# First attention layer: gate projection tiles set into the attention loop, keys projected last ahead of it, one output bank

## The chip, the cores and the metric

The kernel runs on one core of a Trainium2 chip, in one launch. The metric is the device time in microseconds (us); lower is better.

## What is computed

Four transformer layers over 512 tokens of width 1024, all in float32: an NSA layer (sparse attention with three branches), a differential attention layer, a neighbourhood attention layer and an MLA layer, the last two each with a gated side input. The change touches the NSA layer only. Cut to what matters:

```python
u = rmsnorm(x, g)
q, kc, vc, ks, vs, kw, vw, gate, z = split(u @ w_in)     # 16 heads of 64, 4 key groups
k_cmp, v_cmp = compress(kc), compress(vc)                # 31 blocks, a small MLP
o_c = softmax(q k_cmp + bias) v_cmp
o_s = softmax(q ks + bias) vs       # 8 selected blocks of 64 out of 8: all keys
o_w = softmax(q kw + bias) vw       # window 512: all keys
o = sigmoid(gate) . (o_c, o_s, o_w)
y = (o * silu(z)) @ w_out           # z: 1024 columns, from 1024 features
x = x + rmsnorm(y, g2)
```

## The kernel before

Every matrix product is made of three: a float32 operand is split into a high part (ScalarE's Copy into fp32r) and a low part (raw minus high), and hi*lo, lo*hi and hi*hi are added up in PSUM. SBUF holds all activations; weights stream in *units* of 128x2048 (1 MB) into a ring of three slots (`w_raw`, `w_hi`, `w_lo`). The Sync engine (SP) issues a unit's load as soon as the unit that held the slot is consumed; ScalarE (ACT) makes the high part (`split_high`, L417), GpSimd (POOL) the low part (`split_low`, L426), then TensorE (PE) may use it. Every engine runs a program written by hand, in order; semaphores hold them together. The table `RUNS` (L83 on) gives the order of the units.

**The front of the NSA layer** (`block.tensor`, L2331 on): values, then `nsa_k` in two blocks (first the columns to be compressed, then the keys of both full branches), the first half of the compression (`compress_hidden_tensor`, L1794), the queries in two blocks with the second half between them, the gate logits, and `nsa_z` in two blocks. A block of 512 output columns is 96 matmuls of 128x512. Beside the first z block run the scores against the compressed keys (L1905), on VectorE (DVE) and ACT their softmax meanwhile, and in the last part of the second z block their transposes (`compress_turn_tensor`, L1966). `silu_x` (L683) puts silu(z) into `x`.

**The NSA flow** (`pair_tensor` L1354, `pair_vector`, `pair_scalar`, `pair_pool`): 64 steps, one for each pair of heads (8), half of the queries, branch (2) and query tile; a step has two heads (m) and 128, 256, 384 or 512 keys, and eight steps (one pair of heads) repeat. Step i: PE `scores(i)` (6 matmuls, L1360); DVE adds the bias and takes the maximum (L1460); ACT `exps` (L915); DVE the reciprocal (L1466); POOL `normalise` (L1579); PE `turn` (transposes, L1388, banks 4 and 5); ACT `high` (L1518) and DVE `low` (L1473) take the turned maps out as `u_hi` and `u_lo`; PE `values` for two steps at once (L1407; L1415 adds the compressed branch) into bank 6 or 7. Four steps make a group: ACT `low_out` (L1526), DVE `add_out` (L1480), POOL `gate_out` (times silu(z), split; L1586 to L1596). PE's loop takes two steps at a time: at its turn i it does scores i and i+1, turn i-3, the values of steps i-6 and i-5, turn i-2. ACT's loop does at i: exps(i-1), high(i-3), and `low_out` in every fourth. After the flow `nsa_out` multiplies by w_out; its first chunks (`first_output`) already stand in the flow's last turns.

The differential layer behind it has a flow with projection chunks between its own products (`diff_tensor`, `fill`, `tile_product`, L505): tiles of 128 columns of q, k and z, 8 chunks of 3 matmuls each, in banks 2 and 3 by turns.

## Time and profile before

| what | value |
| --- | --- |
| median of 3 runs | 1393.45 us (1392.7 to 1395.8) |
| the profiled execution's own time | 1394.15 us |
| its span, first to last instruction | 1392.2 us |
| granted TensorE clock, mean | 0.997 |
| busy: PE, ACT, POOL, DVE | 1338.4, 732.5, 765.3, 653.7 us |
| NSA front, continuous on PE | from about 28 to 202.6 us |
| NSA flow: first scores to last values | 202.9 to 360.5 us |
| one pair of heads (8 steps) in the flow | 18.6 us |

A busy time of PE counts a matmul from its start to its modelled end, and these overlap: a 128x512 matmul has a busy time of 0.39 us while the next one starts 0.227 us after it. So PE is read by the distance between starts, and a "busy" of 93% leaves more room than it says.

### The profile page before, as it was taken

The numbers are of one execution on the slowest core, as the hardware profiler recorded it, in microseconds if no ns is written. First come the engines' busy times: TensorE is split into PE (matmuls) and PEld (weight loads), VectorE is DVE, ScalarE is ACT, GpSimd is POOL, SyncE is SP. The second block draws the span as 40 slices with busy tenths as digits, with TensorE's granted clock in tenths as the row PEclk, the third lists the DMA queues.
The fourth block names the chain that finished last, engine by engine and source line by source line (L and its number), as shares of the span: only waits on it lengthen the run. The fifth ranks groups of instructions, "written<-read, shape, count | busy, mean of one in ns | idle before, by whom it ended". The sixth has DMA issues, their size and how long they took to land.

```text
span 1392.2 us, 20871 instructions
## 1 busy us (share of the span) xinstructions
PE 1338.4 (96%) x7738; PEld 1096.1 (79%) x7738; DVE 653.7 (47%) x1609; ACT 732.5 (53%) x1552; POOL 765.3 (55%) x771
## 2 busy tenths in 40 slices
PE   6999999999999999999999999999999999999997
PEld 5888777777888787878788888778889887778885
DVE  4222068888251454553420012881463347887135
ACT  4244258888343556665433233892544356887252
POOL 4455256667554465665652544686646433686652
PEclk9999999999999999999999999999999999999999
DMA  6232311100434222221443222425226222002322
GB/s 240 102 118 95 121 61 32 32 32 2 167 113 145 90 76 99 79 96 44 168 152 139 104 91 91 152 92 197 80 93 225 91 91 61 2 16 105 137 91 61
DMA packets 28324, 138.65 MB, mean 100 GB/s; under 512 B 3520, under 2 KB 4032, under 8 KB 16960
## 3 DMA queue, kind: packets, MB, share of 16 engines
q1 hardware_dynamic: 14624, 98.05, 20.0%
q10 hardware_dynamic: 13600, 39.27, 8.2%
q8 instruction: 63, 1.03, 0.3%
q14 instruction: 37, 0.30, 0.1%
HBM read 127.86 MB, written 8.39 MB: 98 GB/s over the span
## 4 chain that ended last, share of the span: by engine, by line
PE 75%; DVE 8%; POOL 6%; ACT 6%; issue 2%; DMA 2%; ACTq 0%; SPq 0%; POOLq 0%; DVEq 0%
PE psum L471 51%; PE psum L505 9%; DVE w_free L1460 2%; POOL w_free L1579 2%; ACT w_free L915 2%; PE psum L1407 2%; PE psum L1029 2%; PE psum L1388 2%; PE psum L1360 2%; PE psum L1003 2%; ACT u_hi L1518 1%; DVE u_lo L1473 1%; PE psum L725 1%; POOL split L1596 1%; PE psum L1373 1%
## 5 line engine op out<-in xcount | busy, mean ns | idle before, releaser
L426 POOL TENSOR_TENSOR w_lo<-w_raw,w_hi 128x2048 fp32r<-128x2048 f32 (+2 forms) x154 | 415.6, 2714 | 317.6 <-ACT w_hi L417 308.3
L417 ACT ACTIVATE w_hi<-w_raw 128x2048 fp32r<-128x2048 f32 (+1 forms) x90 | 167.1, 1856 | 94.7 <-DMA w_raw<-in_weights 79.5
L471 PE MATMUL psum<-w_hi,split 128*128 128x512 f32 x608 | 195.2, 394 | 3.0 <-POOL w_lo L426 2.2
L471 PE MATMUL psum<-u_lo,w_hi 128*128 128x512 f32 (+1 forms) x492 | 194.1, 395 | 0.0
L471 PE MATMUL psum<-u_hi,w_hi 128*128 128x512 f32 (+1 forms) x492 | 191.7, 390 | 0.0
L471 PE MATMUL psum<-u_hi,w_lo 128*128 128x512 f32 (+1 forms) x492 | 191.7, 390 | 0.0
L915 ACT ACTIVATE w_free<-w_free,neg_max 128x512 f32<-128x512 f32 (+3 forms) x256 | 148.4, 585 | 10.1 <-DVE neg_max L1460 9.1
L1473 DVE TENSOR_TENSOR u_lo<-psum,u_hi 128x512 fp32r<-128x512 f32 (+3 forms) x256 | 123.8, 519 | 28.9 <-ACT u_hi L1518 26.2
L471 PE MATMUL psum<-w_hi,u_lo 128*128 128x512 f32 (+2 forms) x352 | 134.6, 382 | 1.8 <-DVE u_lo L875 1.8
L471 PEld LDWEIGHTS psum<-w_hi,split 128*128 128x128 f32 x608 | 114.2, 188 | 27.5 <-POOL w_lo L426 3.1
L471 PE MATMUL psum<-w_lo,u_hi 128*128 128x512 f32 (+2 forms) x352 | 132.9, 378 | 0.0
L471 PE MATMUL psum<-w_hi,u_hi 128*128 128x512 f32 (+2 forms) x352 | 132.8, 377 | 0.0
L1518 ACT ACTIVATE u_hi<-psum 128x512 fp32r<-128x512 f32 (+3 forms) x256 | 107.9, 463 | 41.8 <-PE psum L1388 38.5
L1388 PE MATMUL psum<-ident,w_free 128*128 128x128 f32 x704 | 110.6, 282 | 17.2 <-POOL w_free L1579 8.1
L471 PE MATMUL psum<-w_lo,split 128*128 128x512 f32 x304 | 118.4, 389 | 0.0
L1388 PEld LDWEIGHTS psum<-ident,w_free 128*128 128x128 f32 x704 | 75.7, 140 | 47.7 <-POOL w_free L1579 27.7
L1579 POOL TENSOR_SCALAR w_free<-w_free,inv 128x256 f32<-128x256 f32 (+1 forms) x128 | 73.2, 586 | 64.2 <-DVE inv L1466 64.2
L471 PEld LDWEIGHTS psum<-u_lo,w_hi 128*128 128x128 f32 (+1 forms) x492 | 91.8, 187 | 20.5 <-issue 0.7
L471 PEld LDWEIGHTS psum<-u_hi,w_hi 128*128 128x128 f32 (+1 forms) x492 | 91.8, 187 | 20.1
L471 PEld LDWEIGHTS psum<-u_hi,w_lo 128*128 128x128 f32 (+1 forms) x492 | 91.9, 187 | 19.1
L1407 PE MATMUL psum<-u_lo,split 128*128 128x256 f32 (+1 forms) x416 | 102.9, 284 | 0.0
L1579 POOL TENSOR_SCALAR w_free<-w_free,inv,gate 128x256 f32<-128x256 f32 (+3 forms) x128 | 76.5, 608 | 43.1 <-DVE inv L1466 43.0
(216 smaller groups left out, 2503.6 us busy)
## 6 DMA issues: line engine op xcount, KB each, us to landing
w_raw<-in_weights SPq DMA_DIRECT2D x87, 1024.0 KB, 4.8
x<-x_scratch ACTq DMA_DIRECT2D x12, 512.0 KB, 5.2
gain<-in_gains ACTq DMA_DIRECT2D x9, 512.0 KB, 4.7
gain<-in_strips ACTq DMA_DIRECT2D x16, 256.0 KB, 2.9
spare<-in_strips ACTq DMA_DIRECT2D x16, 256.0 KB, 3.0
x_scratch<-x ACTq DMA_DIRECT2D x8, 512.0 KB, 4.1
gain<-in_near ACTq DMA_DIRECT2D x8, 512.0 KB, 4.3
w_raw<-in_near ACTq DMA_DIRECT2D x8, 512.0 KB, 3.7
```

The costliest lines, as they stand in the source:

```text
L417: high = nc.scalar.activation(w_hi[b][:, c], w_raw[b][:, c], ACT.Copy)
L426: low = nc.gpsimd.tensor_tensor(w_lo[b][:, c], w_raw[b][:, c], w_hi[b][:, c].bitcast(F32), ALU.subtract)
L471: mm = nc.tensor.matmul(dst, lhs, rhs, start=(a == 0 and k == 0 and (wl, ul) == (0, 1)), stop=(a + 1 == u and k + 1 == nk and (wl, ul) == ...
L505: mm = nc.tensor.matmul(bank(tiles.bank(t)), w[b][:, c:c + P], u[:, k * T:(k + 1) * T], start=(k == 0 and nth == 0), stop=(k == KC - 1 and ...
L915: nc.scalar.activation(p_map(f, i, m, n), p_map(f, i, m, n), ACT.Exp, scale=-1.0, bias=stat_of(neg_max, i, m), accum_out=stat_of(row_sum, ...
L1003: mm = nc.tensor.matmul(bank(m, n), lhs, split[64 * m:64 * m + 64, b:b + n], start=(nth == 0), stop=(nth == 2))
L1029: mm = nc.tensor.matmul(head_bank(d, r), turned_place(i, n, low)[:, pt], split[:, a + v:a + v + P], start=(kt == 0 and nth == 0), stop=(kt ...
L1388: tr = nc.tensor.transpose(psum[:, 4 + m, kt * P:(kt + 1) * P], p_map(f, i, m, n)[:, kt * P:(kt + 1) * P], ident[:])
L1407: mm = nc.tensor.matmul(dst, value_place(f, d, m, kt), pt_pair(buf, pt_step(f, 2 * d) // 2, m, a, b), start=(br == 0 and m == 0 and kt == ...
L1473: nc.vector.tensor_tensor(u_lo[:, c], bank(4 + m, n), u_hi[:, c].bitcast(F32), ALU.subtract).then_inc(f.low, 1)
L1518: nc.scalar.activation(u_hi[:, pt_cols(pt_step(f, i), m, n)], bank(4 + m, n), ACT.Copy).then_inc(f.high, 1)
L1579: nc.gpsimd.tensor_scalar(p_map(f, i, m, n), p_map(f, i, m, n), stat_of(inv, i, m), factor_of(f, i, m), ALU.mult, ALU.mult).then_inc(f.p, 1)
```

## The change

- `nsa_k` is cut in two: `nsa_kc` (compressed columns) stays first, then q0, both halves of the compression back to back, the gate logits, q1, and `nsa_k` (keys) last. The compressed scores run beside and behind q1, their softmax while the keys are projected.
- `nsa_z` is no block any more but 8 tiles of 128 columns, 8 chunks of 3 matmuls (128x512) each, all through PSUM bank 7 (`z_fill`). Six chunks stand ahead of the flow; then in each turn of PE's loop one chunk stands behind the scores and one behind the turns. ACT takes a tile out with Silu (`z_take`), between exps(8t+1) and high(8t-1); the next tile's first chunk waits for that (`z_taken`). ACT splits half a unit for each tile (128x1024), POOL two pieces of 128x512.
- The flow's outputs use bank 6 alone (`out_bank`), so a group's values wait for the group before to be added out. The turned maps move to `x` and to ring slots, since u must stay whole for the z tiles; `nsa_out`'s second unit goes to the place of u when z is done. Its first unit is split in four pieces in the last steps of the flow, the second behind it.
- The gate logits' unit is split over 384 columns instead of 2048.

```diff
 _run("nsa_v", 1, (4, 4), 512, "tokens")
-_run("nsa_k", 2, (4, 4), 512, "features")
+_run("nsa_kc", 1, (4, 4), 512, "features")
+_run("nsa_q0", 1, (4, 4), 512, "features")
 _run("nsa_cmp0", 1, (16,), 128, "compress")
-_run("nsa_q0", 1, (4, 4), 512, "features")
 _run("nsa_cmp1", 1, (16,), 128, "compress")
+_run("nsa_gate", 1, (8,), GATES, "features")
 _run("nsa_q1", 1, (4, 4), 512, "features")
-_run("nsa_gate", 1, (8,), GATES, "features")
-_run("nsa_z", 2, (4, 4), 512, "features")
+_run("nsa_k", 1, (4, 4), 512, "features")
+_tiles("nsa_z", [("z", u) for u in range(KC)])
...
+        def out_bank(f, g):
+            return 6 if f is nsa_flow else 6 + g % 2
...
+        Z_FIRST = 6
+        Z_BANK = 7
+        def z_step(t):
+            return max(0, KC * (t + 1) - Z_FIRST - 1) // 2 * 2 + 1
...
+        def z_fill(pe, first, count):
+            b = SLOT[Z_UNIT]
+            for c in range(first, min(first + count, KC * KC)):
+                t, k = divmod(c, KC)
+                if k == 0:
+                    pe.wait_ge(z_ready, t + 1)
+                    if t == 0:
+                        pe.wait_ge(cmp_shifted, 1)
+                    else:
+                        pe.wait_ge(z_taken, t)
+                col = t % 2 * D + k * P
+                for nth, (w, u) in enumerate(((w_hi, u_lo), (w_lo, u_hi), (w_hi, u_hi))):
+                    mm = nc.tensor.matmul(bank(Z_BANK), w[b][:, col:col + P], u[:, k * T:(k + 1) * T], ...)
+                if k == KC - 1:
+                    mm.then_inc(z_done, 1)
...
+        def z_take(act, t):
+            act.wait_ge(z_done, t + 1)
+            if t >= 3:
+                act.wait_ge(nsa_flow.gated, 2 * (t - 2))
+            nc.scalar.activation(z_home(t), bank(Z_BANK), ACT.Silu).then_inc(z_taken, 1)
...
     def values(d, m):
-                if m == 0 and br == 0 and g >= 2:
-                    pe.wait_ge(f.out_sum, 2 * g - 2)
+                held = 1 if f is nsa_flow else 2
+                if m == 0 and br == 0 and g >= held:
+                    pe.wait_ge(f.out_sum, 2 * (g - held) + 2)
...
     in pair_tensor's loop over i = 0, 2, 4, ...
                 for n in steps:
                     scores(n)
+                if f is nsa_flow:
+                    z_fill(pe, Z_FIRST + i, 1)
...
                 if 0 <= i + 1 - LAG < f.steps:
                     turn(i + 1 - LAG)
+                if f is nsa_flow:
+                    z_fill(pe, Z_FIRST + i + 1, 1)
+                    if i == 0:
+                        compress_turn_tensor(pe, 3)
...
     in pair_scalar's loop over i
+                    for t in range(KC):
+                        if t >= 2 and i == z_step(t - 2) + 3:
+                            z_high_part(act, t)
+                    if f.steps - 4 <= i < f.steps:
+                        split_high(act, NSA_OUT, i - f.steps + 4, 4)
                 if 0 <= i - 1 < f.steps:
                     exps(act, f, i - 1)
+                if f is nsa_flow:
+                    for t in range(KC):
+                        if i == z_step(t) + 1:
+                            z_take(act, t)
...
     in pair_pool's loop over i
+                if f is nsa_flow:
+                    for t in range(2, KC):
+                        if i - z_step(t - 2) - 5 in (0, 1):
+                            z_low_part(pool, t, i - z_step(t - 2) - 5)
+                    if f.steps - 3 <= i <= f.steps:
+                        split_low(pool, NSA_OUT, i - f.steps + 3)
+                    if i == f.steps + LAG + 2:
+                        split_low(pool, NSA_OUT + 1)
...
     PE's program
-            project_tensor(pe, "nsa_k")
-            compress_hidden_tensor(pe, 0)
-            project_tensor(pe, "nsa_q0")
-            compress_hidden_tensor(pe, 1)
-            project_tensor(pe, "nsa_q1", between={(0, 0, 2): lambda: compress_heads_tensor(pe)})
-            project_tensor(pe, "nsa_gate", banks=1, base=4)
-            project_tensor(pe, "nsa_z", only=(0,), between=...)
-            project_tensor(pe, "nsa_z", only=(1,), between=...)
+            project_tensor(pe, "nsa_kc")
+            project_tensor(pe, "nsa_q0")
+            compress_hidden_tensor(pe, 0)
+            compress_hidden_tensor(pe, 1)
+            project_tensor(pe, "nsa_gate", banks=1, base=6)
+            project_tensor(pe, "nsa_q1", between=beside_q1)
+            for j in range(NT):
+                compress_scores_tensor(pe, 1, j)
+            project_tensor(pe, "nsa_k")
             pair_tensor(pe, nsa_flow)
```

How the order moves, at three places. **PE in the flow, at its turn i = 8t+2** (L1360 and L1459 are scores, L1388 and L1487 turns, L1407 and L1507 values, L1416 a chunk of z). Before:

```order
L1388 MATMUL psum<-ident,w_free_63 128x128 x6
L1360 MATMUL psum<-split 128x128 x6
L1360 MATMUL psum<-split 128x256 x6
L1388 MATMUL psum<-ident,w_free_63 128x128 x8
L1407 MATMUL psum<-u_lo,split 128x256
```

Now:

```order
L1487 MATMUL psum<-ident,w_free_68 128x128 x6
L1416 MATMUL psum<-u_lo,w_hi_55 128x512
L1416 MATMUL psum<-u_hi,w_lo_59 128x512
L1416 MATMUL psum<-u_hi,w_hi_55 128x512
L1459 MATMUL psum<-split 128x128 x6
L1459 MATMUL psum<-split 128x256 x6
L1416 MATMUL psum<-u_lo,w_hi_55 128x512
L1416 MATMUL psum<-u_hi,w_lo_59 128x512
L1416 MATMUL psum<-u_hi,w_hi_55 128x512
L1487 MATMUL psum<-ident,w_free_68 128x128 x8
```

The first three chunk rows are the last chunk of tile t, the second three the first chunk of tile t+1: the scores of two steps stand between them.

**ACT in the flow, at i = 8t+1 and 8t+2** (L915 and L956 are exps, L1518 and L1630 high, L1526 and L1638 low_out, L1445 the Silu of a z tile). Before:

```order
L1518 ACTIVATE u_hi<-psum 128x384 x2
L1526 ACTIVATE arena<-psum 64x512
L915 ACTIVATE w_free_63,row_sum<-w_free_63,neg_max 128x256 x2
L1518 ACTIVATE u_hi<-psum 128x512 x2
L915 ACTIVATE w_free_63,row_sum<-w_free_63,neg_max 128x128 x2
```

Now:

```order
L1630 ACTIVATE x_r<-psum 128x384 x2
L1638 ACTIVATE arena<-psum 64x512
L956 ACTIVATE w_free_68,row_sum<-w_free_68,neg_max 128x256 x2
L1445 ACT_TABLE_LOAD
L1445 ACTIVATE arena<-psum 128x512
L1630 ACTIVATE x_r<-psum 128x512 x2
L956 ACT_TABLE_LOAD
L956 ACTIVATE w_free_68,row_sum<-w_free_68,neg_max 128x128 x2
```

Behind the same three pieces of work now come a table load and the Silu, and the next exps have a table load of their own.

**ACT in the front**, from q0's last outputs (L604, L645) on; L417 and L467 are high parts of units. Before:

```order
L604 ACTIVATE split<-psum 128x512 x2
L1815 ACT_TABLE_LOAD
L1815 ACTIVATE arena<-arena 128x248
L417 ACTIVATE w_hi_55<-w_raw_61 128x2048
L417 ACTIVATE w_hi_53<-w_raw_59 128x2048
```

Now:

```order
L645 ACTIVATE split<-psum 128x512 x2
L467 ACTIVATE w_hi_56<-w_raw_64 128x384
L467 ACTIVATE w_hi_54<-w_raw_62 128x2048
L1951 ACT_TABLE_LOAD
L1951 ACTIVATE arena<-arena 128x248
L467 ACTIVATE w_hi_55<-w_raw_63 128x2048
L2014 ACT_TABLE_LOAD
L2014 ACTIVATE arena<-psum 48x512
```

The gate unit's split (384 columns) and those of q1's two units (2048) follow one another; before, a block of 96 matmuls stood on PE between any two of the short units.

## Rows read from the trace of the kernel before

**Rows 1.** Busy time by stretch: front, flow, drain (first), one period (second)
```profile
core 0: us, PE busy (x) PEld busy (x) DVE busy (x) ACT busy (x) POOL busy (x), PEclk, DMA share, GB/s
41.94:202.60 160.66, 160.66 (x951) 131.97 (x949) 48.58 (x57) 58.77 (x59) 71.69 (x16) 1.00 0.30 105
202.89:341.60 138.71, 127.88 (x1055) 105.43 (x1054) 117.16 (x449) 121.23 (x376) 97.67 (x160) 0.99 0.08 24
341.60:360.49 18.89, 17.51 (x125) 15.54 (x126) 10.03 (x30) 10.03 (x26) 9.45 (x15) 1.00 0.16 57
...
246.90:265.50 18.60, 17.35 (x146) 14.46 (x146) 15.97 (x60) 16.32 (x52) 13.20 (x22) 1.00 0.10 30
```

**Rows 2.** Chain of waits through the front: start us, us, what
```profile
85.62 3.88 PE psum L1794 x64
89.50 21.98 PE psum L471 x96
...
145.43 1.44 PE psum L1905 x24
...
197.09 0.45 PE psum L1966 x4
```

**Rows 3.** Timeline of PE, part of one period: start us, us, engine line op
```profile
267.10 1.49 PE L1360 MATMUL psum<-split 64*128 64x384 f32 x12
268.52 0.66 PE L1388 MATMUL psum<-ident,w_free 128*128 128x128 f32 x4
...
275.13 1.12 PE L1388 MATMUL psum<-ident,w_free 128*128 128x128 f32 x6 [0.36 <-DVE u_lo L1473]
276.18 0.96 PE L1360 MATMUL psum<-split 64*128 64x128 f32 x12
277.06 1.09 PE L1388 MATMUL psum<-ident,w_free 128*128 128x128 f32 x8
277.91 0.36 PE L1407 MATMUL psum<-u_lo,split 128*128 128x256 f32 x1
...
280.36 0.55 PE L1388 MATMUL psum<-ident,w_free 128*128 128x128 f32 x2
```

**Rows 4.** Timeline of PE inside a projection block
```profile
97.04 0.39 PE L471 MATMUL psum<-u_lo,w_hi 128*128 128x512 f32 x1
97.26 0.39 PE L471 MATMUL psum<-u_hi,w_lo 128*128 128x512 f32 x1
97.49 0.39 PE L471 MATMUL psum<-u_hi,w_hi 128*128 128x512 f32 x1
```

**Rows 5.** Timeline of ACT at the place of the future Silu
```profile
275.68 1.09 ACT L1518 ACTIVATE u_hi<-psum 128x384 fp32r<-128x384 f32 x2 [0.18 <-PE psum L1388]
276.80 0.59 ACT L1526 ACTIVATE arena<-psum 64x512 f32<-64x512 f32 x1
277.42 0.51 ACT L915 ACTIVATE w_free<-w_free,neg_max 128x256 f32<-128x256 f32 x1
...
278.54 1.09 ACT L1518 ACTIVATE u_hi<-psum 128x512 fp32r<-128x512 f32 x2
```

**Rows 6.** Timeline of ACT in the differential layer's flow, around one Silu
```profile
503.39 1.92 ACT L417 ACTIVATE w_hi<-w_raw 128x2048 fp32r<-128x2048 f32 x1
505.33 1.28 ACT L1203 ACT_TABLE_LOAD   x1
506.62 0.60 ACT L1203 ACTIVATE x<-psum 128x512 f32<-128x512 f32 x1
...
507.73 1.28 ACT L1175 ACT_TABLE_LOAD   x1
```

**Rows 7.** Timeline of all engines behind the compression's first half
```profile
91.02 1.92 ACT L417 ACTIVATE w_hi<-w_raw 128x2048 fp32r<-128x2048 f32 x1 [4.76 <-DMA w_raw<-in_weights]
93.02 9.18 POOL L426 TENSOR_TENSOR w_lo<-w_raw,w_hi 128x2048 fp32r<-128x2048 f32 x2 [6.13 <-ACT w_hi L417]
94.41 1.92 ACT L417 ACTIVATE w_hi<-w_raw 128x2048 fp32r<-128x2048 f32 x1 [1.48 <-DMA w_raw<-in_weights]
```

**Rows 8.** Timeline of DVE, adding out a group; of POOL, a 512-column low part
```profile
277.43 0.86 DVE L1480 TENSOR_TENSOR arena<-psum,arena 64x256 f32<-64x256 f32 x2
...
385.64 1.30 POOL L426 TENSOR_TENSOR w_lo<-w_raw,w_hi 128x512 fp32r<-128x512 f32 x1 [1.48 <-DVE x L864]
```

**Rows 9.** Chain of waits through the drain of the flow
```profile
349.20 2.82 PE psum L471 x12
...
358.66 1.83 PE psum L1407 x16
360.49 21.86 PE psum L471 x96
```

More of the change, by code:

```diff
@@ L213, in _program @@
         LAG = 3
+        PT_SET = 14 * P
         MLA_SCALE = (64 + ROPE) ** -0.5
@@ L1352, in scores @@
             def scores(i):
-                if f is nsa_flow and i < 2:
-                    pe.wait_ge(bank_free["act"], 4 + RUNS["nsa_out"]["others"] - 2 + 2 * i)
+                if f is nsa_flow and i == 0:
+                    pe.wait_ge(bank_free["dve"], 4 + RUNS["nsa_k"]["taken"] + 4)
                 if i >= 2:
@@ L1548, in pair_scalar @@
                     high(i - LAG)
-                if i == (f.steps if f is na_flow else f.steps + LAG - 1) and f is not nsa_flow:
+                if i == (f.steps if f is na_flow else f.steps + LAG - 1):
                     split_high(act, RUNS[f.name + "_out"]["unit"] + 1)
@@ L2405, in _ @@
             load_strips(act, nsa_flow, 1)
-            project_scalar(act, "nsa_z", silu_x, only=(0,))
+            project_scalar(act, "nsa_q1", split_features_act(QH + 4 * T, 0.125), halves=True, split_at=1)
             compress_softmax_scalar(act)
-            last_z_scalar(act, "nsa_z", silu_x)
+            z_high_part(act, 0)
+            z_high_part(act, 1)
+            for j in range(NT):
+                act.wait_ge(bank_done, 4 * RUNS["nsa_k"]["block"] + j + 1)
+                nc.scalar.activation(split[:, KH + j * T:KH + (j + 1) * T], bank(j), ACT.Copy).then_inc(split_hi, 1)
+            for g in range(3):
+                compress_turned_high(act, g)
             pair_scalar(act, nsa_flow)
```

241 lines of the change are left out of this document (153 added, 88 removed).

## Prediction

> **What bounds the kernel now.** I read the busy times by stretch first. In the front PE is busy for the whole stretch and the others for less than half [rows 1], and the chain of waits runs through PE alone, block after block [rows 2]: there only PE's work counts. In the flow a period of eight steps takes 18.6 us, with ACT busy for 16.32, DVE 15.97 and POOL 13.20 us of it [rows 1]. PE's busy time (17.35) has to be read by the distance of starts. From the timeline of PE [rows 3]: scores of 384 and 512 keys take 1.42 us (267.10 to 268.52), of 128 and 256 keys 0.88 us (276.18 to 277.06); 8 transposes 0.85 us; 20 value matmuls 2.45 us (277.91 to 280.36), 0.122 each. A period holds two of each kind of scores (4.6 us), 40 transposes (4.2) and 56 value matmuls (6.9): 15.7 us. So PE stands idle for some 2.9 us of a period, 17 us in the six regular periods, in pieces behind DVE and POOL such as the 0.36 us at 275.13 [rows 3]. That is the room into which the change puts z.
>
> **What leaves the front.** Two blocks of 96 matmuls, at 0.227 us from start to start [rows 4]: -43.6 us, all on PE's path. Six chunks of three return ahead of the flow: +4.1 us. One of four groups of transposes (0.45 us [rows 2]) moves into the flow. The other projections, compressed scores (1.44 us a set [rows 2]) and transposes only change places. The softmax that ran beside z has the keys' block (21.8 us) and the six chunks as its cover.
>
> The new order has one place where a unit is late. The compression's halves and the gate logits now follow one another: 3.88 + 3.88 + 24 x 0.227 = 13.2 us on PE from 85.6, so it is ready for q1 at 98.8. q1's first unit takes the slot freed by the first half, at 89.5. In the trace such a load landed at 94.4, its high part took 1.92 us and its low part 4.6 us (9.18 for two) [rows 7]: 100.9. PE waits 2.1 us. For q1's second unit the same chain ends under q1's first half. Front in all: -43.6 + 4.1 - 0.45 + 2.1 = **-37.9 us**.
>
> **What enters the flow.** 58 chunks. A chunk costs 3 x 0.227 = 0.68 us of PE, eight in a period 5.5 us: PE's own work is 15.7 + 5.5 = 21.2 us, already over 18.6. ACT gets one Silu (0.60 us), two table loads (1.28 us each, as around the Silu in the differential flow [rows 6]) and a high part of 128x1024 (bounded by 0.6 and 1.92 us, half of the latter taken, 1.0): 4.2 us, so 20.5 us of work. POOL gets two pieces of 1.30 us [rows 8]: 15.8 us, still covered. DVE gets nothing.
>
> To that comes a new wait. All tiles use bank 7. The last chunk of tile t is issued behind turn(8t-2), the first of tile t+1 two scores later, and waits for the Silu. In between ACT has to work through high(8t-2), low_out, exps(8t+1), a table load, the Silu. In the trace, from the end of that turn (PE goes on at 276.18 [rows 3]) to the end of exps(8t+1) (278.54 [rows 5]) it is 2.36 us; with 1.28 + 0.60 it is 4.24 us. PE can put one chunk (0.69) and the scores (0.88) into it. It waits 2.7 us, with the semaphore 2.8 us. More slack on ACT would not shorten this, because high(8t-2) cannot start before the turn. Behind the Silu ACT in turn waits about a microsecond for chunk and turn(8t-1). A period becomes 21.2 + 2.8 = **24.0 us**. I walked PE and ACT through one period with these durations, and nothing else ended later: the maps for each turn are ready 1 to 4 us ahead. The waits that PE has now vanish under the chunks.
>
> One output bank: values of a new group wait for add_out. Now the adding ends at 278.29 [rows 8], just behind the values' start at 277.91 [rows 3]; with two to three chunks and the wait for the Silu between, the bank is free before it is wanted. Cost 0, with the chunks as cover; without them about 0.4 us in every second group.
>
> **The sum.** Before: 138.7 us from the first scores to scores 62 and 63, then 18.9 us of drain [rows 1]. Now: the opening up to turn 6 of the loop about 13.3 us (8.6 us of scores, transposes and six chunks, a first wait of 2.8 for a Silu, some 2 us in which turn(2) waits for what ACT and DVE still owe to turn(1); before it was 8.5, the 138.7 less seven periods), six periods of 24.0 = 144.0, then the last period with 4 chunks instead of 8 and no wait for a bank, but Silu and table loads on ACT (19.5 us of work there), 20: 177.3 us, +38.6. In the drain POOL has four more pieces of 1.30 us ahead of the first `nsa_out` chunks, which stood there without a stall [rows 9]; they hold PE for about 3 us, of which the drain's own idle time takes back a good part: +1.7 us. The low part of the second unit (4.6 us) lies under the last values and output chunks and ends about 1.5 us before it is needed. Behind the flow all is as it was. -37.9 + 38.6 + 1.7 = **+2.4 us**. Against the profiled execution's own 1394.15 us that is 1396.5; the median shown is 0.7 us lower, so I predict **1395.8 us**. A measurement of this kernel tells a change from none at about 0.2% (2.8 us); this is just inside.
>
> **The rivals.**
> *The cover holds (faster).* If the wait for bank 7 falls into time that PE would lose anyway, a period is PE's work or ACT's, 21.2 or 20.5 us, and with small change 21.5. That takes 2.5 us from each of six periods and from the opening: 17 us less, 1378 us. For it: ACT has now 2.3 us idle in a period and could run ahead. Against it: the chain begins with a turn that PE issues right before its own last chunk. Chance 0.2.
> *ACT becomes the clock (slower).* ACT has 20.5 us of work, and its present waits (18.6 - 16.3 = 2.3 us) are for turns which the chunks make later, not earlier. If they stay, and the wait for turn(8t-1) behind the Silu, with its own chunk and transposes (1.5 to 2 us) and the one bank's 0.4 to 1 us come on top, a period takes 25.5 to 26 us: +11 us in six periods and the opening, 1407 us. It decides from the point at which ACT has no idle time left but behind turns. Chance 0.2.
> *A table load costs more than its record.* In the differential flow the Silu starts 1.29 us after its table load [rows 6], with no gap before the load either: the high part of 1.92 us ends where it starts. If a switch drained ACT for about as long again, each wait would be 1.3 us longer, with seven waits +9 us: 1405 us. Chance 0.02, since these rows show no drain. The Trainium skill ("ScalarE: Activation LUTs", "What ACT_TABLE_LOAD costs") states such a rule: 1283 ns for the load and some 1380 ns of drain, 2.66 us for every switch, and under "Table sets" it says to batch calls by set. By that price the sum would be +12 instead of +2.4 us; the trace agrees with its 1283 ns and not with its drain.
> *The change does not do what it says.* Each engine's order shows the chunks, loads and splits at the places named, so this is not it.
>
> **How the numbers follow.** The walk as it stands: 0.58, with a span of its own of 1390 to 1402 (a wait of 2.5 to 3.3 us seven times, opening and drain 2 us either way, the late unit 0 to 3 us). Of it 0.04 lies below 1390.6, 0.33 within 0.2% of before, 0.21 above. Cover 0.2, all faster; ACT as clock 0.2 and drain 0.02, all slower. So faster 0.24, same 0.33, slower 0.43: the likeliest time lies within the bound, but more of the chance lies above it. The range takes in both large rivals, cut at their near sides: 1379 to 1409.
>
> **What would show it.** PE should reach the flow's first scores near 165 us with one wait of about 2 us for a low part ahead of q1 (L426's counterpart). In the flow seven waits of PE on the Silu of bank 7, 2.5 to 3.3 us each, at a distance of 24 us; ACT with 16 more table loads there and busy for about 20.5 of 24 us; no wait of values on the adding. The last values should end about 2 us later than the 360.5 us of now [rows 9]. The theory is wrong if the waits on the Silu are under a microsecond, if the periods are 21.5 us (cover) or 26 us (ACT), or if the front gains less than 36 us.

## The result, and the profile after

The changed kernel takes **1425.17 us** (median of four runs, 1422.79 to 1431.29) against 1394.62 us in the same session: ratio 1.0226, 95% interval 1.0188 to 1.0264. I had predicted 1395.8 us and a range of 1379 to 1409. The profiled execution took 1422.79 us, with a span of 1421.0 us and a mean granted clock of 0.986 (before: 1394.15, 1392.2 and 0.997). Here and below, times are medians and ratios come from the runs' means, without four slow runs far out (4604.56 us of spread_cmp, 1642.04 us of no_fill, 2641.24 and 1494.69 us of the kernel before).

By stretches, busy times of the changed kernel: front, flow from the first scores to scores 62 and 63, drain, one period at full clock, one with a stretch at half clock (the columns are those of [rows 1]):

```profile
41.94:167.71 125.77, 123.74 (x774) 101.79 (x774) 50.79 (x54) 40.50 (x44) 49.45 (x14) 0.97 0.27 93
167.71:359.91 192.20, 169.18 (x1232) 140.19 (x1232) 120.27 (x451) 152.59 (x405) 109.12 (x170) 0.96 0.13 45
359.91:387.40 27.49, 22.25 (x126) 18.69 (x126) 11.15 (x32) 14.09 (x33) 16.81 (x21) 0.81 0.12 39
207.92:233.18 25.26, 22.25 (x170) 18.42 (x170) 16.20 (x61) 20.43 (x55) 15.77 (x24) 1.00 0.13 42
233.18:260.04 26.86, 23.84 (x170) 19.86 (x170) 16.31 (x61) 20.65 (x55) 15.74 (x24) 0.94 0.13 41
```

| stretch, us | before | predicted | after | miss |
|---|---|---|---|---|
| to the first scores of the flow | 202.89 | 165.0 | 167.71 | +2.7 |
| opening, to scores 6 and 7 | 9.2 | 13.3 | 13.31 | 0 |
| six periods | 110.8 | 144.0 | 157.86 | +13.9 |
| last period | 18.6 | 20.0 | 21.02 | +1.0 |
| drain | 18.9 | 20.6 | 27.49 | +6.9 |
| all behind | 1031.8 | 1031.8 | 1033.6 | +1.8 |

(The opening of before is counted here to the same scores, 6 and 7; my 8.5 us was what 138.7 us leave beside seven whole periods.) Of the 26.3 us of miss, 21.8 stand in the loop and its drain. The 1.8 us behind them come with a stretch of 3.4 us at half of TensorE's clock at 487.1 us, in the next layer, where the trace of before has none. The 0 in the opening is luck: PE waits 0.8 us at its second turn where I had counted some 2, but scores, transposes and chunks take 9.7 us where I had counted 8.6.

**The wait is there, in the size predicted.** PE's waits from the first scores to scores 62 and 63:

```profile
PE psum L1416 <- ACT arena L1445: 11.0, 4, 2.7
PE psum L1416 <- ACT x L1445: 8.3, 3, 2.8
PE psum L1487 <- DVE w_hi L1582: 2.2, 8, 0.8
PE psum L1487 <- DVE w_lo L1582: 0.9, 2, 0.6
```

Seven waits for the Silu, 19.3 us, 2.76 each. One of them and what follows, in the timeline of PE:

```profile
270.14 0.47 PE L1416 MATMUL psum<-u_lo,w_hi 128*128 128x512 f32 x1
270.46 0.39 PE L1416 MATMUL psum<-u_hi,w_lo 128*128 128x512 f32 x1
270.68 0.40 PE L1416 MATMUL psum<-u_hi,w_hi 128*128 128x512 f32 x1
271.01 0.95 PE L1459 MATMUL psum<-split 64*128 64x128 f32 x12
274.71 0.47 PE L1416 MATMUL psum<-u_lo,w_hi 128*128 128x512 f32 x1 [2.75 <-ACT arena L1445]
275.01 0.40 PE L1416 MATMUL psum<-u_hi,w_lo 128*128 128x512 f32 x1
275.25 0.40 PE L1416 MATMUL psum<-u_hi,w_hi 128*128 128x512 f32 x1
275.48 1.88 PE L1487 MATMUL psum<-ident,w_free 128*128 128x128 f32 x8
277.01 0.56 PE L1507 MATMUL psum<-w_hi,split 128*128 128x256 f32 x1
```

Two things stand here that the sum did not have. **The chunk** of three matmuls at 270.14 holds PE until 271.01: 0.87 us, not 0.68. The starts are 0.32, 0.22 and 0.33 us apart: only between matmuls of a kind is it the 0.227 of [rows 4]; the first, behind transposes, and the step to the scores take a tenth of a microsecond more each. A chunk behind scores holds it for about 0.80. Eight chunks are 6.7 us, not 5.5. **The clock**: the eight transposes at 275.48 take 1.53 us to the next start, where the same eight took 0.85 [rows 3]. Windows at that place, at the four sets of compressed scores in front, and in the drain (the granted clock is the third column from the right):

```profile
275.50:278.90 3.40, 3.40 (x18) 3.40 (x17) 1.57 (x4) 2.08 (x3) 0.73 (x2) 0.50 0.02 5
...
135.50:142.30 6.80, 6.80 (x41) 5.99 (x40) 3.64 (x4) 0.00 (x0) 0.00 (x0) 0.50 0.10 39
367.60:377.80 10.20, 8.13 (x28) 6.73 (x29) 2.64 (x6) 3.57 (x8) 9.83 (x12) 0.50 0.01 2
```

The granted clock fell to half (1.2 of 2.4 GHz) behind four of the seven waits in the flow. A period without such a stretch takes 25.26 us, one with it 26.81 to 26.86, so each costs 1.6 us. The chain of waits through the front shows the late unit of q1 as predicted (the low part lands, and PE goes on at 101.22 after a wait of 1.8 us), and four sets of compressed scores in 6.84 us, mostly at half clock, in place of 4 x 1.44 us [rows 2]:

```profile
85.90 3.90 PE psum L1930 x64
89.80 0.02 issue
89.82 4.74 DMA w_raw<-in_weights
94.56 0.02 issue
94.58 1.92 ACT w_hi L467
96.51 0.07 issue
96.57 4.60 POOL w_lo L478
...
131.73 6.84 PE psum L2042 x96
```

**The drain** is the same work with a new queue. The timeline of POOL:

```profile
365.02 1.28 POOL L478 TENSOR_TENSOR w_lo<-w_raw,w_hi 128x512 fp32r<-128x512 f32 x1 [4.22 <-ACT w_hi L467]
366.29 1.31 POOL L1703 TENSOR_SCALAR w_free<-w_free,inv,gate 128x384 f32<-128x384 f32 x2
367.56 1.27 POOL L478 TENSOR_TENSOR w_lo<-w_raw,w_hi 128x512 fp32r<-128x512 f32 x1
368.82 1.52 POOL L1703 TENSOR_SCALAR w_free<-w_free,inv,gate 128x512 f32<-128x512 f32 x2
```

POOL's first low piece of `nsa_out` (its step 61) waits 4.22 us, because ACT counts the unit's high part up only with its fourth piece, at ACT's step 63. The probability rows of steps 60 and 61 stand behind it, then rows and pieces alternate. PE, which waits for these rows and last for the fourth piece:

```profile
367.00 1.55 PE L1487 MATMUL psum<-ident,w_free 128*128 128x128 f32 x6 [2.65 <-POOL w_free L1703]
369.64 1.97 PE L1487 MATMUL psum<-ident,w_free 128*128 128x128 f32 x8 [1.08 <-POOL w_free L1703]
374.14 0.80 PE L523 MATMUL psum<-w_hi,split 128*128 128x512 f32 x1 [0.94 <-POOL w_lo L478]
```

### The profile page after: what moved, and what is told of

It reads as the page before. It is cut to its first block, busy times and chain, and to the rows that moved or that the text cites. A ratio compares the mean times of both kernels' runs of the same rounds, so it can differ in the third digit from the quotient of the medians.

```text
span 1421.0 us, 20936 instructions
## 1 busy us (share of the span) xinstructions
PE 1348.3 (95%) x7738; PEld 1104.6 (78%) x7738; DVE 660.5 (46%) x1609; ACT 749.8 (53%) x1572; POOL 765.4 (54%) x786
## 4 chain that ended last, share of the span: by engine, by line
PE 78%; DVE 7%; ACT 6%; POOL 4%; issue 2%; DMA 2%; ACTq 0%; SPq 0%; POOLq 0%; DVEq 0%
PE psum L523 47%; PE psum L557 9%; PE psum L1487 3%; PE psum L1416 3%; PE psum L1459 3%; PE psum L1507 3%; DVE w_free L1570 2%; PE psum L1070 2%; PE psum L1044 1%; ACT w_free L956 1%; POOL w_lo L478 1%; PE psum L766 1%; PE psum L1472 1%; POOL w_free L1703 1%; DVE arena L910 1%
## 5 line engine op out<-in xcount | busy, mean ns | idle before, releaser
L478 POOL TENSOR_TENSOR w_lo<-w_raw,w_hi 128x512 fp32r<-128x512 f32 (+3 forms) x153 | 392.6, 2581 | 277.3 <-ACT w_hi L467 267.8
L467 ACT ACTIVATE w_hi<-w_raw 128x2048 fp32r<-128x2048 f32 (+1 forms) x89 | 158.5, 1781 | 89.4 <-DMA w_raw<-in_weights 75.5
L523 PE MATMUL psum<-u_lo,w_hi 128*128 128x512 f32 (+1 forms) x428 | 169.6, 396 | 2.0 <-POOL w_lo L478 2.0
L523 PE MATMUL psum<-u_hi,w_lo 128*128 128x512 f32 (+1 forms) x428 | 167.5, 391 | 0.0
L523 PE MATMUL psum<-u_hi,w_hi 128*128 128x512 f32 (+1 forms) x428 | 167.5, 391 | 0.0
L956 ACT ACTIVATE w_free<-w_free,neg_max 128x512 f32<-128x512 f32 (+3 forms) x256 | 148.3, 584 | 11.3 <-DVE neg_max L1570 10.2
L1487 PE MATMUL psum<-ident,w_free 128*128 128x128 f32 x704 | 109.9, 285 | 14.8 <-POOL w_free L1703 8.2
L1487 PEld LDWEIGHTS psum<-ident,w_free 128*128 128x128 f32 x704 | 80.9, 144 | 37.8 <-POOL w_free L1703 16.8
L523 PEld LDWEIGHTS psum<-u_lo,w_hi 128*128 128x128 f32 (+1 forms) x428 | 80.3, 188 | 20.8 <-POOL w_lo L478 2.7
L523 PEld LDWEIGHTS psum<-u_hi,w_hi 128*128 128x128 f32 (+1 forms) x428 | 80.2, 187 | 17.8
L523 PEld LDWEIGHTS psum<-u_hi,w_lo 128*128 128x128 f32 (+1 forms) x428 | 80.3, 188 | 16.7
L1459 PE MATMUL psum<-split 64*128 64x512 f32 (+3 forms) x768 | 86.6, 349 | 4.9 <-DVE neg_max L1570 4.4
L1459 PEld LDWEIGHTS psum<-split 64*128 64x128 f32 x768 | 56.7, 185 | 31.4 <-DVE neg_max L1570 17.0
L557 PE MATMUL psum<-u_lo,w_hi 128*128 128x512 f32 x192 | 78.3, 408 | 0.0
```

The lines of the kernel that those rows point to most:

```text
L467: high = nc.scalar.activation(w_hi[b][:, c], w_raw[b][:, c], ACT.Copy)
L478: low = nc.gpsimd.tensor_tensor(w_lo[b][:, c], w_raw[b][:, c], w_hi[b][:, c].bitcast(F32), ALU.subtract)
L523: mm = nc.tensor.matmul(dst, lhs, rhs, start=(a == 0 and k == 0 and (wl, ul) == (0, 1)), stop=(a + 1 == u and k + 1 == nk and (wl, ul) == ...
L557: mm = nc.tensor.matmul(bank(tiles.bank(t)), w[b][:, c:c + P], u[:, k * T:(k + 1) * T], start=(k == 0 and nth == 0), stop=(k == KC - 1 and ...
L956: nc.scalar.activation(p_map(f, i, m, n), p_map(f, i, m, n), ACT.Exp, scale=-1.0, bias=stat_of(neg_max, i, m), accum_out=stat_of(row_sum, ...
L1459: mm = nc.tensor.matmul(score_place(f, i, m), *products[m][nth], start=(nth == 0), stop=(nth == 2 and f is not mla_flow))
```

## The experiments

Thirteen kernels, each compared with the kernel before in its own session. All start from the changed kernel. "Turn" below is PE's loop index, which goes by two. The stretches of the table above are used throughout.

### One cost at a time

**late_chunk**: the chunk that opens a tile goes behind the turned products.

```diff
-                if f is nsa_flow:
+                if f is nsa_flow and i % 8 != 2:
                     z_fill(pe, Z_FIRST + i, 1)
...
-                    z_fill(pe, Z_FIRST + i + 1, 1)
+                    z_fill(pe, Z_FIRST + i + (i % 8 != 2), 1 + (i % 8 == 2))
```

> The chunk that opens a gate tile (behind the scores of turns 2, 10, 18 ...) is moved behind the turned products of the same turn, where two chunks now stand; nothing else. Theory (the wait for the tile before is what TensorE pays, and the half clock follows from it): the seven waits of 2.76 us at the opening chunk (19.3 us) shrink to under 2 us in all, and the four stretches at half clock behind them (4 x 1.57 us = 6.3) go with them, so about 1425.2 - 17.5 - 6.3 = 1401 us; a period between two scores of the same tile place falls from 25.3 or 26.8 to 22.6 us. Rival 1 (ScalarE with its two table loads a tile is the clock of the loop): it has the same work, so the period stays over 25 us and the time within 3 us of 1425. Rival 2 (the half clock has another cause than the wait): the waits go and the stretches stay, 1407 to 1408 us.

Measured: 1408.1 us, ratio 1.0101 (1.0074 to 1.0128), 7 us above the theory and at the time of rival 2, but not by its mechanism. Of the seven waits one of 0.9 us is left, and in the six periods no half clock: they take 142.7 instead of 157.9 us. ScalarE is not the clock: a period falls to 23.76 us with ACT's 20.3 us of work unchanged. But not to 22.6: PE now waits 14 times for low parts that VectorE writes to `w_lo`, where in the changed kernel it waited twice (the row for `w_hi`, the other place of the same line, stays at 2.2 us):

```profile
PE psum L1487 <- DVE w_lo L1582: 6.1, 14, 0.6
```

The chunk behind the scores was the cover of that wait. That is the 1.2 us a period that are missing. The drain takes 28.05 us, and half clock stands in the profile at other places: 10.2 instead of 6.8 us in front, 3.4 in the opening, 13.7 instead of 10.2 in the drain, 6.8 instead of 3.4 in the layers behind. So the mean granted clock of the profiled run is still 0.986, and front, opening, drain and what is behind are together 3.2 us longer than in the changed kernel.

**pairs**: no chunk behind scores, two behind the turned products of each turn (`z_fill(pe, Z_FIRST + i, 2)`).

> Both chunks of each turn stand behind the turned products, six matmuls in a row, and none behind the scores; the opening chunk of a tile is thereby late as in the run before. Theory (a chunk costs 0.80 to 0.87 us instead of 0.68 because its first matmul behind an instruction of another kind takes 0.31 and the change back costs as well): a pair costs 1.5 us instead of 1.67, so four times 0.17 a period and seven periods, about 5 us less than the run with the opening chunk alone moved: 1396 us. Rival (the chunk behind the scores covers TensorE's wait for GpSimd's rows): without it the wait for turned products returns behind the scores, up to 0.7 us a turn, and this run is not faster than the one before, 1401 to 1415 us.

Measured: 1401.87 us, ratio 1.0057 (1.0042 to 1.0072). The period is 22.9 us, and in the six periods the waits for VectorE's low part in `w_lo` are down from 5.2 to 1.8 us: 3.4 of the 5.2 us between this run's six periods (137.5) and late_chunk's (142.7). The gain is about the one expected (the 1396 us expected stood on a late_chunk of 1401), but the waits account for more of it than the saved changes of kind do; the rival, that waits return, is out, though the time lies in its range.

**copy_gate**: `ACT.Silu` in `z_take` becomes `ACT.Copy` (the gate is z itself, so computation is changed), nothing else.

> The gate tiles are copied instead of passed through Silu (computation changed: the outputs carry z itself), so that ScalarE loads no table in the loop. Theory (the wait of 2.76 us at the opening chunk holds the table load of 1.28 us ahead of the Silu, the other load stands behind it and costs TensorE nothing): seven waits of 1.4 to 1.5 us, 9 us less, ScalarE busy 18.0 instead of 20.6 us a period, half-clock windows behind fewer of the waits, 1412 to 1416 us. Rival 1 (ScalarE is the clock): the period falls by both loads, 2.6 us, 1407 us or less. Rival 2 (the wait is for the exponentials in front, not the load): under 3 us comes back.

Measured: 1405.5 us, ratio 1.0078 (1.0051 to 1.0106). The waits, from the flow's start to the end of the drain:

```profile
PE psum L1416 <- ACT arena L1445: 5.8, 4, 1.5
PE psum L1416 <- ACT x L1445: 4.3, 3, 1.4
```

1.44 us each instead of 2.76: 1.3 us less, one table load, and a full-clock period is 24.0 instead of 25.26. This is the test of the price per switch: were there a drain of its own beside the load, each wait would have lost more than the load. The Trainium skill ("ScalarE: Activation LUTs", "What ACT_TABLE_LOAD costs") puts such a drain at some 1380 ns; the trace shows none here. The time lies in the range of rival 1, but a period fell by one load, not by both. I had the time too high by 7 to 10 us. By the profiles the run is 17.6 us shorter: 9.2 us are the waits and 4.7 the half clock behind them (in the six periods one stretch is left, at 194.1 us, right behind a wait of 1.45 us, and none in the five periods after it); 1.1 us are the last period, and 2.5 the drain, with 6.8 instead of 10.2 us at half clock.

**no_fill**: the chunks' matmuls are left out, and Silu reads another tile (computation left out).

```diff
                 if k == KC - 1:
-                    mm.then_inc(z_done, 1)
+                    pe.sem_inc(z_done, 1)
...
-            nc.scalar.activation(z_home(t), bank(Z_BANK), ACT.Silu)
+            nc.scalar.activation(z_home(t), u_hi[:, 0:T].bitcast(F32), ACT.Silu)
```

> The 64 chunks of the gate projection are left out (computation left out: the gate is Silu of another tile); ScalarE's Silu, its table loads, the weights' loads and splits and the single output bank stay. Theory: the attention begins 4.1 us earlier (six chunks), a period loses 6.7 us of chunks and 2.8 us of wait, but with ScalarE busy 20.6 us a period of 18.6 (as before the change) can't return: 20.6 to 21.3 us, ScalarE being the clock only now; the drain keeps GpSimd's queue, 24 to 27 us; in all 1425 - 4.1 - 4 - 6 x 5 - 2 = 1385 us (1380 to 1390). Rival (the one output bank or ScalarE set the 25 us period of the change): the period stays above 23 us, 1398 us or more.

Measured: 1401.25 us, ratio 1.0042 (1.0027 to 1.0058): 16 us slower than I expected, with a period of 23.6 to 24.1 us and not one chunk in it. What I had overlooked in my own edit is that PE's wait for the Silu stays in `z_fill`, and with less work ahead of it, it is longer. Timeline of PE:

```profile
233.42 0.96 PE L1455 MATMUL psum<-split 64*128 64x128 f32 x12
237.79 1.94 PE L1483 MATMUL psum<-ident,w_free 128*128 128x128 f32 x8 [3.42 <-issue]
```

Timeline of ACT:

```profile
235.77 1.28 ACT L1441 ACT_TABLE_LOAD   x1
237.06 0.63 ACT L1441 ACTIVATE x<-u_hi 128x512 f32<-128x512 f32 x1
```

Window behind the wait (columns as above):

```profile
237.79:243.00 5.21, 5.21 (x26) 5.21 (x26) 2.13 (x7) 3.36 (x7) 2.37 (x5) 0.51 0.00 0
```

PE stands for 3.42 us (the view names no releaser, but the Silu ends at 237.69). Half clock comes with all six such waits, for 6.8 us in five of them (it sets in before the wait has ended, so some 5 us of it fall on work) and for 3.4 in one. So without any chunk the loop takes longer than `pairs` with all of them (142.9 against 137.5 us): a wait of 3.4 us, with the clock behind it, costs a period more than its eight chunks do. That is again the time of the rival, and not its mechanism: PE waits for the Silu, not for the bank of the outputs (next run), and `pairs` has a period of 22.9 us with about the same work on ACT (20.3 us). The Trainium skill ("TensorE: Matmul & The Clock Gate", "HAM oscillation — how this bites in real kernels") describes this pattern, a wait in every round of a loop behind which the round starts at half rate. The trace agrees in six cases of six where the wait is 3.4 us, in four of seven at 2.76 us, and in one of seven at 1.44 us (copy_gate).

**no_fill_2banks**: no_fill, with outputs alternating between banks 6 and 7 again (`return 6 + g % 2`, `held = 2`).

> As no_fill, and the outputs of the attention alternate between two banks as in the kernel before. Theory (one output bank costs nothing): the same time as no_fill within 1 us. Rival (the bank is held until VectorE has read it, 0.3 us at each group or more where the loop is faster): 16 groups by 0.3 to 1 us, 5 us or more faster than no_fill.

Measured: 1403.9 us, ratio 1.0059 (1.0037 to 1.0081), against no_fill's 1.0042 (1.0027 to 1.0058). The second bank gives nothing back (profiled spans 1399.7 and 1400.2 us).

**drain_early**: ACT's four high pieces of `nsa_out` stand two at step 60 and two at 61.

> ScalarE takes the first half of the output weights in pieces two at step 60 and two at 61 instead of one at each of steps 60 to 63; GpSimd's order is unchanged. Theory (GpSimd's first low piece waits for the last of the four, and the rows of step 60 and 61 stand behind it): the low piece starts at about 361 instead of 365.0 us, the wait of 4.22 us on GpSimd is under 1 us, the waits of 2.65 and 1.08 us of the turned products go, and with them at least half of the 10.2 us at half clock: 4 to 7 us off the stretch from the scores of steps 62 and 63 (359.9) to the end of the values (387.4), so 1418 to 1421 us. Rival (the stretch is bound by GpSimd's own sum of low pieces, scaled rows and gates): under 1.5 us comes back, 1424 to 1425 us.

Measured: 1423.55 us, ratio 1.0205 (1.0188 to 1.0222). POOL's wait for the high part went from 4.22 us to nothing at that piece, and the drain from 27.49 to 24.43 us with 3.4 instead of 10.2 us at half clock. That is less than the 4 to 7 us expected, and the time did not come down to 1418 to 1421 us. In the profile front and loop gave it back: the clock fell at six of the seven waits instead of four (opening 14.7, six periods 159.6 us). Up to the drain this program is the changed kernel, so at which of these waits the clock falls is not fixed by the program; the four runs of the changed kernel have mean clocks of 0.979 to 0.986, too. Still 5.5 us above the drain of before: PE waited 2.2 us for the last low piece.

**spread_cmp**: of the compressed scores' second half one set stands in each column block of the keys' first half, by `between` of `project_tensor`.

> The compressed scores of the second half of the heads stand one set in each column block of the keys' first half, instead of four sets in a row ahead of it. Theory (four sets in a row, small matmuls of 32 columns, are where the granted clock fell to half at 135.5 to 142.4 us): no half clock there, sets of 1.44 us, first scores of the attention at about 164.7 instead of 167.7 us, so 1425.2 - 3 = 1422 us. Rival 1 (the softmax, which ends 8 us later, is then late for its turn): TensorE waits 1 to 3 us at the turn of the compressed rows, and nothing comes back, 1424 to 1426 us. Rival 2 (the clock falls wherever these sets stand): the half clock moves into the keys' block and nothing comes back.

Measured: 1422.87 us, ratio 1.0203 (1.0186 to 1.022). No half clock in front any more, first scores at 165.56 us; but it fell at 172.9 us, in the opening (14.84 us instead of 13.31). That this is the price of the move is not shown: in drain_early, late_chunk and pairs, whose front is that of the changed kernel, it fell at 174.5 to 174.8 us as well. At the end of the drain 0.4 us are left, at the end of the profile 0.1. The softmax was not late.

### Taking the faults out together

**fix_pairs_drain**: pairs and drain_early, and the four low pieces made by VectorE at its steps 64 and 65.

> Pairs behind the turned products, as in the run pairs; ScalarE's pieces of the output weights early, as in drain_early; and their four low pieces by VectorE at its steps 64 and 65 instead of GpSimd's at 61 to 64. Theory (in the drain GpSimd holds rows back with low pieces of 1.28 us each, and the output product, whose weights are whole only with the fourth, holds back the values behind it): the wait for the low piece (2.2 us in drain_early) and the waits for rows (1.2) go, the drain from the scores of 62 and 63 to the end of the values is 20 to 22 us instead of 27.7, with no or one half-clock window in it, so 1401.9 - 6.5 = 1395 us, within 2 us of the kernel before. Rival (VectorE's pieces hold back its own low parts instead): the drain stays over 24 us and the time over 1398.

Measured: 1400.15 us, ratio 1.0039 (1.0026 to 1.0053), 5 us above the time expected. The drain is 22.5 us (20 to 22 expected), without half clock; the opening was 1.2 us longer, by half clock. Still 2.1 us of wait for the last low piece.

**fill_fixed**: pairs from turn 2 on, none at turn 0; ACT's high pieces early; two low pieces by POOL behind the rows of step 59 and two by VectorE; spread_cmp; the first gate tile made in front, and an Exp of one column behind the keys' outputs, which loads the table for the loop there.

```diff
+            beside_k = {(0, 0, j): (lambda j: lambda: compress_scores_tensor(pe, 1, j))(j) for j in range(NT)}
+            beside_k.update({(0, 1, j): (lambda j: lambda: z_fill(pe, 3 * j, 3 if j < 2 else 2))(j) for j in range(3)})
...
+                    if i >= 2:
+                        z_fill(pe, Z_FIRST + i, 2)
```

> Four changes together. The compressed scores of the second half stand in the keys' first half, as in spread_cmp. The first gate tile (8 chunks) is made between the keys' last columns and passed through Silu while ScalarE is idle there, so nothing is filled at turns 0 and 1 and no Silu stands in the opening; the loop's chunks stand in pairs behind the turned products. Of the output weights' low pieces GpSimd makes two after the rows of step 59 and VectorE two at its step 64. Theory, from the profiled run of fix_pairs_drain (1397.9 us): the opening up to the scores of 6 and 7 falls from 15.7 us to 11 or 12 (the wait of 0.9, the half clock behind it, one pair of 1.5 us less) while 1.4 us of matmuls go to the front; the front gives back 2.2 us or more; the drain loses the wait of 2.1 us for the low pieces; in all 6 to 8 us less, 1390 to 1392 us by the profile and 1392 to 1394 us median, faster than the kernel before by 0.1 to 0.2%. Rival (what stands behind the front takes it back: rows of the compressed branch late, a half clock in the opening as in spread_cmp): the same 1398 to 1400 us as fix_pairs_drain.

Measured: 1397.73 us, ratio 1.0019 (1.0007 to 1.0031), where I had expected 1392 to 1394. The drain is down to 20.1 us. Two new waits stand in front: 3.2 us of the first chunk for the softmax to have read bank 7, and 2.3 us of the last compressed turn for VectorE.

**fill_fixed2**: two of those sets in q1's last columns, two in the keys' first.

> As fill_fixed, but of the compressed scores of the second half two sets stand in the last columns of q1 and two in the first two column blocks of the keys, so that the softmax ends some 6 us earlier. Theory (the two waits that fill_fixed took on, 3.2 us for the softmax's read of bank 7 and 2.3 us for the turned rows of the compressed branch, come from the late softmax alone): both are gone, and with them at least one of the half-clock windows at 153.6 and 174.1 us (1.5 us each, 6.8 us long the second); first scores at 166 to 167.5 us instead of 171.0, opening 12 to 13.5 us instead of 14.7, loop and drain as before (137.3, 20.7, 20.1 us): 1395.7 - 5.5 - 1.5 to 3 = 1387 to 1389 us by the profile, 1389 to 1391 us median, 0.4% faster than the kernel before. Rival (two more sets of small matmuls close together bring the clock down there, or the opening is bound by the chain from scores through softmax rows to the turn whatever the gate does): 1393 us or more.

Measured: 1398.27 us, ratio 1.0021 (1.0009 to 1.0034): not faster, and 7 us above what I had expected. The wait of 3.2 us went, the one of 2.3 us stayed, so the late softmax was not its cause: the turn needs its bank back from copy and low part of the three turns before, and the chunks at turn 0 had been its cover. Half clock came at 101, 128, 135 and 176 us.

**fill_first** and **fill_first2**: pairs from turn 0 on (`Z_FIRST = 8`), the sets in a row (fill_first) or as in fill_fixed2 (fill_first2).

> As fill_fixed, but the compressed scores of the second half stand four sets in a row again, and the pairs of chunks begin at turn 0 (the second gate tile), so that the last pair stands at turn 54. Theory (the wait of 2.3 us ahead of the last turn of the compressed rows is one that a pair of chunks covers, and the waits of 3.2 us in front came from the late softmax): both are gone; the front keeps its half clock at the four sets (first scores 169 to 170 us); the opening takes 13 us or less, six periods 137.3, the last 19.5 instead of 20.7, the drain 20.1: 169.5 + 13 + 137.3 + 19.5 + 20.1 + 1031.9 = 1391.3 us by the profile, 1392 to 1394 us median. Rival (the opening costs 14.7 us by the half clock whatever stands in it): 1393.5 us by the profile, 1396 median, no faster than the kernel before.

> As fill_first, with the compressed scores placed as in fill_fixed2 (two sets in the last columns of q1, two in the first of the keys). Theory of placement (four sets of small matmuls in a row cost a half-clock window): 1.5 to 3 us faster than fill_first, 1389 us by the profile. Rival (the half-clock windows in front come with two sets in a row as well, as in fill_fixed2 at 128 and 135 us): the same as fill_first within 1 us.

Measured: 1400.25 us, ratio 1.0038 (1.0026 to 1.005), and 1401.69 us, ratio 1.0049 (1.0035 to 1.0064): both miss their expectations by 6 us and more. The wait ahead of the turn is 0.7 us, but six periods are 142.2 instead of 137.2 us: a period of 23.79. With the fill one turn earlier the Silu stands two steps earlier on ACT (8t, not 8t+2). Timeline of ACT in fill_first:

```profile
239.42 1.28 ACT L1446 ACT_TABLE_LOAD   x1
240.71 0.60 ACT L1446 ACTIVATE x<-psum 128x512 f32<-128x512 f32 x1
241.21 1.08 ACT L1635 ACTIVATE x_r<-psum 128x512 fp32r<-128x512 f32 x2
```

And of PE:

```profile
242.67 1.12 PE L1488 MATMUL psum<-ident,w_free 128*128 128x128 f32 x6 [1.08 <-DVE w_hi L1580]
```

Table load and Silu take 1.9 us. ACT's copy of the turned rows starts 1.81 us behind the end of the exponentials (239.40); in fill_turn2 (next), with no Silu at this step, the same copy waits for its rows only and starts 0.91 us behind them:

```profile
234.80 1.09 ACT L1636 ACTIVATE x_r<-psum 128x512 fp32r<-128x512 f32 x2 [0.91 <-PE psum L1488]
```

So the copy is 0.9 us late, VectorE's low part behind it too, and PE waits 1.08 instead of 0.20 us in each period. The placing of the compressed scores gained nothing by the medians; by the profiles fill_first2 reaches the first scores 4.2 us earlier, but fill_turn2, with the same front as fill_first, does so 3.7 us earlier, with 6.8 instead of 13.7 us at half clock.

**fill_turn2**: as fill_first, but turn 2 gets no pair (`if i != 2:`), so that the Silu is back at step 8t+2.

> As fill_first, but turn 2 is left without a pair of chunks, so that from turn 4 on the chunks and ScalarE's Silu stand at the steps at which they stand in fill_fixed (Silu at step 8t+2 instead of 8t), and the pair at turn 0 stays. Theory (the 0.9 us a period that fill_first lost, 23.79 against 22.88 us, come from ScalarE's copies of turned rows held back by the Silu and its table loads at a step with 384 keys, not from the fill): the wait for VectorE's low part behind the Silu goes back to under 0.3 us a period, six periods to 137.3 us, and the opening stays at 13 us or less: 5 us less than fill_first, 1395 to 1396 us median, the same as the kernel before within 0.1%. Rival (the pair at turn 0 or the first tile in front costs it): six periods stay at 142 us and the time at 1400.

Measured: **1394.6 us**, ratio 1.0004 (0.999 to 1.0018). Flow, drain and one period:

```profile
169.02:339.99 170.97, 163.88 (x1225) 134.57 (x1226) 120.96 (x451) 149.99 (x406) 109.29 (x170) 0.99 0.14 47
339.99:360.08 20.09, 17.91 (x126) 15.53 (x126) 11.92 (x34) 13.12 (x32) 15.25 (x19) 1.00 0.15 52
204.90:227.78 22.88, 22.31 (x169) 18.50 (x168) 16.31 (x61) 20.33 (x55) 15.78 (x24) 1.00 0.16 47
```

Compared with fill_first, the six periods take 137.2 instead of 142.2 us and nothing else in them has moved but the step of fill and Silu. The medians are 5.7 us apart, the ratios 0.0034 (4.7 us). Against the kernel before, by the profiles (1391.9 and 1392.2 us): front -33.9, opening +3.8, six periods +26.4, last period +2.1, drain +1.2, behind +0.1 us. With the faults found taken out the change breaks even; I found no version that is faster than the kernel before. One chunk costs 0.54 us in the loop ((22.88 - 18.60) / 8), 0.68 in front. That difference, some 6 us in six periods (48 chunks are 32.7 us by the price in front and add 26.4), is all that PE's idle time was worth there, and the rest uses it up. In front the moved work alone would be 38.6 us less (43.6 out, 5.4 back for eight chunks, 0.45 for the transposes moved); 4.7 of that are lost to the late unit of q1 (a wait of 1.7 us) and to half clock at the compressed scores. The drain is 1.2 us longer. Opening and last period hold four chunks each (2.7 us by the price in front), so together they lose 0.5 us.

## Why the prediction was wrong

By its own steps, with what the runs put in their place:

- **Front, -37.9 us**: -35.2. Blocks, chunks and the late unit of q1 (predicted 2.1 us of PE's time) came as worked out. Missing, 2.7 us, was the half clock at the four sets of compressed scores, which I had let "only change places"; spread_cmp, without it, reaches the first scores 2.15 us earlier.
- **"A chunk costs 3 x 0.227 = 0.68 us"**: the term that was mis-sized. 0.80 to 0.87 us at single places between other kinds, 1.2 us a period, over 7 us in six. The spacing I used was taken inside a block of equal matmuls [rows 4], where no change of kind occurs.
- **"PE stands idle for some 2.9 us of a period, 17 us in the six regular periods"**: that is 18.6 less a sum of spacings, so it holds the changes of kind too. The waits that the profile of before names for PE in these six periods sum to 5.8 us. The sum of the prediction did not use the 17 us, but the hope behind the change did.
- **The wait for bank 7, 2.8 us seven times**: right, 2.76. late_chunk, copy_gate and no_fill show that it is the chain high part, exponentials, table load, Silu, and not ACT's total work.
- **Period 24.0 us**: 25.26 with the chunk's real price (24.0 + 1.2), 26.86 where the clock fell. The failed step is that I priced each wait by its length. The walk took every duration from rows at full clock, although the trace of before has a stretch of half clock too (clock 0.99 in the flow [rows 1]). Four of them cost 6.3 us here. In the periods of the eight kernels without a wait for the Silu there (late_chunk, pairs and all of the second group), 48 in all, not one stretch stands. Why the clock falls at one wait of 2.76 us and not at the next, the runs leave open.
- **One output bank, cost 0**: right. PE waits once, 0.3 us, in the drain, and no_fill_2banks gains nothing even without chunks as cover.
- **Drain, "+1.7 us; four more pieces ... hold PE for about 3 us"**: the step that failed outright, +8.6. I added up POOL's work and did not ask what its first piece waits for and what stands behind it. The first piece waited 4.22 us for the unit's last high piece, with the rows of two steps behind it, and 10.2 us then ran at half clock. drain_early, without that wait, took 3.1 us off; with the pieces shared between POOL and VectorE the drain is 20.1 us.
- **"More slack on ACT would not shorten this"**: true of the wait. But I had taken ACT for the rest as covered, and fill_first against fill_turn2 shows that the same Silu two steps earlier costs 0.9 us a period on another path.
- **The rivals.** "The cover holds" had the period at 21.5 us, and even without the wait it is 22.9. "ACT becomes the clock", nearest in time with its 1407 us, is refuted as a mechanism: ACT worked 20.4 us of 25.3, and without the wait the period fell at once, to 22.9 us in pairs. The drain of a table load did not show. The time was outside of all of them because three separate misses (chunk, clock, drain) all had one sign; my range was made from alternatives to the sum and took in only 0.5 us a wait for errors within it.

## What to carry to other kernels

When work is filled into an engine's idle time, don't only add durations: look at what each filled piece waits for, and put the piece that opens a shared buffer where its release has long come, since a wait of about 3 us costs its length and here, in 27 cases of 33, a stretch at half clock besides (1.6 us each at 2.76 us). Take the price of a matmul from a place where its neighbours are of another kind, if that is where it will stand. And at the end of a loop, where an engine's queue gets new pieces with a wait at their head, list what is behind that head: there a late piece costs all that queue at once.

## What the runs showed that I had not expected

- A loop with no fill and a wait of 3.42 us in each period (no_fill, 23.8 us a period, 6.8 us of each at half clock) is slower than one with 24 matmuls of 512 columns more and no such wait (pairs, 22.9 us).
- At the same wait of 2.76 us the clock fell four times of seven in one kernel, five of seven in a second (spread_cmp) and six of seven in a third (drain_early), whose loops are the same; at waits of 3.42 us twelve times of twelve (no_fill, no_fill_2banks), at waits of 1.44 us once in seven.
- Four sets of matmuls of 32 columns in a row (96 in 6.84 us, with PE never idle) have a stretch at half clock in all ten kernels that keep them in a row; with one set in each column block (spread_cmp, fill_fixed) it is gone at that place. Other stretches then stand at 153.9 and 174.4 us (fill_fixed) or 172.9 us (spread_cmp), but five kernels with the sets in a row have one at 173 to 176 us too; of the 2.2 us that spread_cmp won in front 0.4 us were left at the end of its drain.
